# Summing ten modulation chunks on VectorE beside two projections, a narrower band mask and a one-step negated maximum

## The reference

```python
def modulation(cvec, w_ada, b_ada):            # w_ada: 1024 x 3072, layer 4: 1024 x 6144
    return jnp.split(jax.nn.silu(cvec) @ w_ada + b_ada, 3, axis=-1)

sh_l, sc_l, gt_l = modulation(c, w_ada, b_ada)       # latent tokens
sh_c, sc_c, gt_c = modulation(c_ctx, w_ada, b_ada)   # context tokens
h_l = rmsnorm(x_lat, g_pre) * (1.0 + sc_l[:, None, :]) + sh_l[:, None, :]
...
# window layers: 16 heads of 64, 4 key heads; |query - key| <= 128 among latents, all context keys
m = jnp.maximum(jnp.max(logits, axis=-1, keepdims=True), sink)
e = jnp.exp(logits - m)
return e / (jnp.sum(e, axis=-1, keepdims=True) + jnp.exp(sink - m))
```

## Time and profile before

| what | us |
| --- | --- |
| median of the timed runs (3) | 2514.43 (2513.34 to 2514.76) |
| the profiled execution | 2511.64 |
| its span | 2509.8 |
| TensorE busy in the span | 2363.6 (94%) |
| VectorE busy | 935.3 (37%) |
| ScalarE busy | 633.5 (25%) |
| projection of layer 0, from tile 4 on | 69.7 to 182.8 |
| attention of layer 0 | 183.8 to 312.5 |
| projection of layer 3, from tile 4 on | 1036.7 to 1109.3 |
| attention of layer 3 | 1110.2 to 1191.9 |

### The profile page before, as it was taken

How to read it: one execution, slowest core, us unless ns; L and a number is a source line. 1 busy time by engine, 2 the same in 40 slices (tenths; PEclk the granted TensorE clock), 3 DMA queues, 4 the chain that set the end, 5 groups by cost and what they waited for, 6 DMA issues and landing times. The chain is left out here.

```text
span 2509.8 us, 31515 instructions
## 1 busy us (share of the span) xinstructions
PE 2363.6 (94%) x11828; PEld 1264.7 (50%) x11829; DVE 935.3 (37%) x2112; ACT 633.5 (25%) x1450; POOL 45.8 (2%) x57
## 2 busy tenths in 40 slices
PE   7999899999999989999899789999999999999997
PEld 3545586468745557675786553333333333333332
DVE  2208643153600684436354433233223223322323
ACT  3016532343211353225331421111111111111111
POOL 0000000000000000000001000000000000000000
PEclk9999999999999999999999789999999999999999
DMA  9028921200122002249231049998998998998997
GB/s 337 34 90 316 350 79 42 72 32 34 68 68 73 28 2 101 101 147 356 68 135 67 21 194 369 417 417 343 417 417 348 417 417 348 418 418 350 418 418 306
DMA packets 154252, 568.00 MB, mean 226 GB/s; under 512 B 10832, under 2 KB 12368, under 8 KB 121136
## 3 DMA queue, kind: packets, MB, share of 16 engines
q1 hardware_dynamic: 154160, 566.75, 57.7%
HBM read 565.67 MB, written 1.05 MB: 226 GB/s over the span
## 5 line engine op out<-in xcount | busy, mean ns | idle before, releaser
L2495 PE MATMUL PS<-BIG,PW 128*64 128x512 f32 x2304 | 510.9, 598 | 11.0 <-DMA BIG<-in_w 10.9
L2495 PEld LDWEIGHTS PS<-BIG,PW 128*64 128x64 f32 x2304 | 160.8, 137 | 357.9 <-issue 322.1
L2521 PE MATMUL PS<-BIG,PW 128*64 128x512 f32 x1152 | 255.1, 595 | 8.6 <-ACT PW L2598 8.6
L2684 DVE TENSOR_SCALAR PW<-PS 128x512 f32<-128x512 f32 x36 | 24.9, 691 | 515.1 <-PE PS L2495 515.1
L2595 ACT ACTIVATE PW<-PW 128x512 f32<-128x512 f32 x36 | 22.7, 630 | 759.1 <-DVE PW L2684 759.1
L2521 PEld LDWEIGHTS PS<-BIG,PW 128*64 128x64 f32 x1152 | 79.3, 137 | 161.3 <-issue 144.1
L973 PE MATMUL PS<-HT,BIG 128*128 128x512 f32 (+1 forms) x448 | 154.0, 502 | 0.0
L619 PE MATMUL PS<-HT,BIG 128*128 128x256 f32 x640 | 139.5, 379 | 2.1 <-PEq L730 2.1
L619 PEld LDWEIGHTS PS<-HT,BIG 128*128 128x128 f32 x640 | 121.4, 190 | 19.1 <-issue 2.7
L973 PEld LDWEIGHTS PS<-HT,BIG 128*128 128x128 f32 x448 | 85.6, 191 | 62.6 <-issue 56.9
L1306 PE MATMUL PS<-BIG,HT 128*128 128x512 f32 x256 | 110.0, 592 | 0.0
(11 more groups left out here) (463 smaller groups left out, 3102.6 us busy)
## 6 DMA issues: line engine op xcount, KB each, us to landing
BIG<-in_w SPq DMA_DIRECT2D x384, 1024.0 KB, 15.8
BIG<-in_l_w_ada SPq DMA_DIRECT2D x24, 2048.0 KB, 9.2
BIG<-in_l_w_in SPq DMA_DIRECT2D x20, 2048.0 KB, 8.1
BIG<-in_w_ada SPq DMA_DIRECT2D x12, 2048.0 KB, 9.9
BIG<-in_l_w_out SPq DMA_DIRECT2D x8, 2048.0 KB, 10.0
BIG<-in_w_in SPq DMA_DIRECT2D x7, 2048.0 KB, 8.5
BIG<-in_w_out SPq DMA_DIRECT2D x2, 2048.0 KB, 7.8
BIG<-in_l_w_in SPq DMA_DIRECT2D x1, 1792.0 KB, 13.4
```

The costliest lines, as they stand in the source:

```text
L2495: ins = nc.tensor.matmul(PS[64 * g:64 * g + 64, 4 + half, :], xt[:, c % 4, c // 4, :], W[:, c, half * F + g * 512:half * F + g * 512 + 512 ...
L2521: ins = nc.tensor.matmul(PS[64 * g:64 * g + 64, 7, :], at_[:, k % 4, k // 4, :], W[:, 8 + k // 2, k % 2 * D + g * 512:k % 2 * D + g * 512 ...
```

## The change

1. **Ten chunks of each attention's modulation move into the projection block ahead of it.** Their weights no longer pass through the ring: SyncE loads them into two places of the arena (`load`), a load waiting until the chunk two before is summed. VectorE multiplies each 128-row slice k with a column of the condition and adds up over k (`sum_rows`): in layer 0 two rows per chunk (16 operations of 128x512), in layer 3 one row in two halves (8 operations). It does so in portions between its rope steps and after the key copies. TensorE adds over the partitions with a column of ones (`reduce`, four matmuls of 256 columns), each reduction at a fixed place behind a tile. The attention keeps ten late chunks in layer 0 and two in layer 3.
2. **The band mask** is added only to the 128 of 256 latent keys where it can be other than 0. The last layer's mask keeps its width.
3. **The negated maximum** with the sink is one operation, min(-scale x max, -sink), with the negated sink made once per attention.

```diff
+                if j >= 2:
+                    sp.wait_ge(*at("early_summed", j - 1))
+                sp.dma_start(self.places[j], t[ADA[l]][:, c * CH:(c + 1) * CH].rearrange("(k p) n -> p k n", p=P)).then_inc(
+                    S[f"early_loaded{j % 2}"].sem, 16)
...
+            def sum_rows(self, dve, a, b):
+
+                for x in range(a, b):
+                    j, k = x // KT, x % KT
+                    two = self.job[j][0] < 4
+                    if k == 0:
+                        dve.wait_ge(*at(f"early_loaded{j % 2}", 16 * (j // 2 + 1)))
+                        if j >= 2:
+                            dve.wait_ge(*at("early_reduced", j - 1))
+                    for h in range(2) if two else [k % 2]:
+                        sums = PART[:, j % 2, h, :]
+                        w, c = self.places[j][:, k, :], 27 + (h if two else 2)
+                        if k == 0 or (k == 1 and not two):
+                            ins = nc.vector.tensor_scalar(sums, w, COND[:, k, c:c + 1], None, ALU.mult)
+                        else:
+                            dve.wait_ge(dve_chain.sem, self.mark[h])
+                            ins = nc.vector.scalar_tensor_tensor(sums, w, COND[:, k, c:c + 1], sums, ALU.mult, ALU.add)
+                        if k == KT - 1 and h == 1:
+                            ins.then_inc(S["early_summed"].sem, 1)
...
+            def reduce(self, pe, j):
+                pe.wait_ge(*at("early_summed", j + 1))
+                for h in range(2):
+                    row = 3 * j + (h if self.job[j][0] < 4 else 2)
+                    for half in range(2):
+                        g = 32 * (2 * h + half)
+                        ins = nc.tensor.matmul(PS[g:g + 32, self.bank, 0:256], UNIT[:, 31 - row:63 - row],
+                                               PART[:, j % 2, h, half * 256:half * 256 + 256], start=(j == 0),
+                                               stop=(j == self.early - 1), tile_position=(0, g))
+                ins.then_inc(S["early_reduced"].sem, 1)
...
-                    x = j * (slots - 2 - 2 * self.batches) // len(self.job) + 2 * b
+                    x = 3 + (j - self.early) * (slots - 8) // late
...
+                pool_chain.link(pool, nc.gpsimd.memset(UNIT[:], 0.0))
+                pool_chain.add(nc.gpsimd.memset(UNIT[:, 31:32], 1.0))
...
                         if sink is not None:
                             h = 2 * units[i][0]
-                            dve_chain.link(dve, nc.vector.scalar_tensor_tensor(
-                                mx[:, i % 2, 2:4], mx[:, i % 2, 0:2], scale, sink[:, h:h + 2], ALU.mult, ALU.max))
-                            nc.vector.tensor_scalar(nm[:, i % 2, 0:2], mx[:, i % 2, 2:4], -1.0, None, ALU.mult).then_inc(
-                                S["max_ready"].sem, 1)
+                            nc.vector.scalar_tensor_tensor(nm[:, i % 2, 0:2], mx[:, i % 2, 0:2], -scale, minus_sink[:, h:h + 2],
+                                                           ALU.mult, ALU.min).then_inc(S["max_ready"].sem, 1)
...
+            sums_beside = [2, 1, 2, 1] + [4] * 6 if i == 0 else [0] * 4 + [3] * 4 + [8] * 2
+            reduced_behind = [4, 6, 8, 10, 13, 15, 16, 17, 19, 20] if i == 0 else [8, 9, 10, 12, 13, 15, 17, 18, 20, 21]
...
+                    if pending:
+                        ws.load_until(sp, first)
+                        for j in range(EARLY):
+                            mods.load(sp, j)
+                            if j in (3, 5):
+                                ws.load_until(sp, first + (j - 1) // 2)
+                    else:
+                        ws.load_until(sp, first - 1)
+                        mods.load(sp, 0)
+                        mods.load(sp, 1)
+                        ws.load_until(sp, first + 1)
+                        mods.load(sp, 2)
+                        sp.wait_ge(*done[3])
+                        for j in range(3, 6):
+                            mods.load(sp, j)
+                        ws.load_until(sp, first + 2)
+                        for j in range(6, EARLY):
+                            mods.load(sp, j)
                     ws.load_until(sp, first + 5)
...
                         if 1 <= j <= len(roped):
                             rope(j - 1)
+                        if j in reduced_behind:
+                            mods.reduce(pe, reduced_behind.index(j))
...
                         act.wait_ge(*done[j])
+                        if kind == "z" and m == 0 and not pending:
+                            act.wait_ge(*at("early_summed", 2))
...
+                    x = 0 if pending else 4
+                    mods.sum_rows(dve, 0, x)
                     for n, j in enumerate(roped):
                         kind, m, _, _, _ = tiles[j]
                         dve.wait_ge(*at("tile_taken", j + 1))
                         rope_turn(dve, (qt if kind == "q" else kt_)[:, m, :], n, tmp)
+                        mods.sum_rows(dve, x, x + sums_beside[n])
+                        x += sums_beside[n]
...
+                    mods.sum_rows(dve, x, KT * EARLY)
...
+            def masked(u):
+                x = P - u[1] * P
+                return (x, window[:, u[1], x:x + P]) if u[1] < 2 else None
```

More of the change, by code:

```diff
@@ L255, in layers_and_experts_kernel @@
                 ws.add("l1_w_ukv", t["l1_w_ukv"])
[L256 to L259, removed]
+            for l, c in {0: [(2, 2), (3, 0)], 3: [(4, EARLY)]}.get(i, []):
+                ws.add(ADA[l], t[ADA[l]][:, c * CH:])
+                ws.first[ADA[l]] -= c
             ws.add(f"l{i}_w_out", t[f"l{i}_w_out"])
@@ L265, in layers_and_experts_kernel @@
         ws.first["end"] = len(ws.chunks)
[L267 to L272, removed]
+        BESIDE = {0: [(l, c) for l in range(4) for c in range(4 if l == 0 else 0, 6)], 3: [(4, c) for c in range(12)]}
         dve_chain = Chain(ctx.enter_context(nc.semaphore("dve_chain")))
@@ L297, in layers_and_experts_kernel, with __init__, ring @@
         class Modulations:
-            def __init__(self, job, rows, bank, batch):
+            def __init__(self, job, rows, bank, batch, early=0, places=None):
                 self.job, self.rows, self.bank, self.batch = job, rows, bank, batch
-                self.end = job[-1][2] + 1
+                self.early, self.places, self.mark = early, places, [0, 0]
                 self.batches = -(-len(job) // batch)
+            def ring(self, j):
+                l, c = self.job[j]
+                return ws.first[f"l0_w_ada_{c}"] if l == 0 else ws.first[ADA[l]] + c
@@ L345, in take @@
                 while j < end:
-                    l, c, _ = self.job[j]
+                    l, c = self.job[j]
                     n = 1
-                    while j + n < end and self.job[j + n][0:2] == (l, c + n):
+                    while j + n < end and self.job[j + n] == (l, c + n):
                         n += 1
@@ L499, in layers_and_experts_kernel @@
         early = consts_at["eps"][1]
-        low, high = ([(0, c, ws.first[f"l0_w_ada_{c}"]) for c in cs] for cs in ((0, 2), (1, 3)))
-        mods = Modulations(low, arena.take(256), 7, 2)
+        mods = Modulations([(0, 0), (0, 2)], arena.take(256), 7, 2)
         w_first = BIG[:, RING_N + ARENA_N - KT * CH:].rearrange("p (k n) -> p k n", k=KT)
@@ L733, in _ @@
                 def _(sp):
-                    ws.load_until(sp, mods.end if mods else ws.done)
+                    ws.load_until(sp, mods.ring(len(mods.job) - 1) + 1 if mods else ws.done)
                 @block.tensor
@@ L873, in modulate @@
                                 mods.take(dve, j)
+                    if sink is not None:
+                        dve_chain.link(dve, nc.vector.tensor_scalar(minus_sink, sink, -1.0, None, ALU.mult))
                     maxima(0)
@@ L2223, in hybrid_mixer @@
             ws.done = c_in + 8
-            attention(units, 0.125, score, value, lambda u: dilated[:, u[1], 0:(u[1] + 1) * P], None, gate)
+            attention(units, 0.125, score, value, lambda u: (0, dilated[:, u[1], 0:(u[1] + 1) * P]), None, gate)
             first = ws.first["w_out_2"]
```

54 lines of the change are left out of this document (39 added, 15 removed).

## The result

The changed kernel takes 2536.1 us (median of 4 runs, 2528.47 to 2540.33), the kernel before beside it 2513.89: ratio 1.0088 [1.006, 1.0117], 22.2 us slower. The profiled execution is the fastest of the four, 2528.47 with a span of 2526.4; that of before had 2509.8.

What follows compares the result with a forecast made beforehand. TensorE was taken to bound the kernel. Projections +24.8 and +21.2, attentions -17.8 and -18.3, clock +5 made +15 on the profiled 2511.64, 2526.5; with 2.8 to the median, 2529 us, range 2511 to 2543.

Steps and rivals of the forecast that it cites:

- the four stages: Projection and attention of layers 0 and 3: +24.8, -17.8, +21.2, -18.3 us, with +5 for low clock, together +15.
- The waits: TensorE's queue in both projections stands at reductions until VectorE's last sum: 20.1 us in layer 0, 16.5 in layer 3.
- Loads bind in layer 3: Layer 3's projection: two load places, 7.9 us issue to landing, hold up the sums; +21.2 us, +15 without that limit.
- A reduction: Ten per projection in TensorE's queue, 0.47 us each, 4.7 us per projection; at most twice that.
- The clock: Low TensorE clock after three long waits, 2 to 2.5 us each: +5, bounds 0 and 8; chance 8 in 10.
- The attentions: Attentions of layers 0 and 3, ten chunks fewer each and shorter VectorE units: -17.8 and -18.3 us.
- The sums: VectorE's multiply-and-add operations beside the projections: 0.66 us start to start; a chunk 10.0 us in layer 0, 4.8 in layer 3.
- It cancels: Attentions give 22 and 20 us, layer 3's loads do not bind, clock stays: -2, 2512; chance 0.20.
- The attentions fall to TensorE's own work: TensorE's waits for VectorE ahead of the transposes vanish, all idle 10.4 and 6.8 us: -14.7, 2500; chance 0.12.
- Clearly slower: Projections: clock falls at every long wait, reductions cost double or sums 0.7 us: +25 to +30, 2541; chance 0.16.
- my sum: The prediction's main case for the whole kernel: 2529 us, range around it alone 2521 to 2538; chance 0.52.

Runs made afterwards that it cites:

- Experiment 3: The changed kernel with each reduction put a few tiles later, nothing else: 2512.78 us, ratio 0.9999 to the kernel before.
- experiment 8: The changed kernel with later reductions, ten chunks in both layers, and layer 3's z weights issued ahead of loads 2 to 9: 2508.96 us, ratio 0.9983.
- experiment 5: The changed kernel with unneeded filler matmuls ahead of the long waits (4, 4, 7, 1 in layer 0; 4, 4, 4 in layer 3): 2531.83 us, ratio 1.0076.
- experiment 10: The changed kernel run and profiled once more, unaltered: 2536.77 us, ratio 1.009 to the kernel before.

## Why the prediction was right, and where its sizes were off

It forecast 2529, slower, in a range of 2511 to 2543; measured were 2536. Sign and mechanism are right; the four stages sum to +22.0 where it had +15.

- **The waits** ("the step that decides"). Forecast 0.9, 4.3, 4.3, 6.9, 2.6, 1.1 us in layer 0; the trace has 0.81, 4.15, 4.15, 6.82, 0.90, 0.36. The brackets count from the end of the rope's matmul; counted by starts, as the forecast did, the long ones are 4.3. The two short ones came out shorter as slower tiles had made TensorE later. In layer 3 two of 4.15 and one of 4.44, at the chunk whose load was held up. In layer 3's later part, where the forecast had 7.9 us of waits in six pieces, they came as 4.44 and 0.28. Experiment 3 shows that in layer 0 the waits are the loss: 23.0 of the 30.2 us go with the places alone.
- **Loads bind in layer 3.** Forecast, and shown twice: experiment 3 takes away the early waits and gains 1.2 us there, experiment 8 ends in waits of 5.31 and 7.01, while eight chunks have none. The forecast put layer 3 without that limit at +15; with eight chunks and the later places of the reductions it is +5.6, since the early waits go as well. That the z weights came early enough held in the changed kernel only because the waits had delayed the tiles.
- **A reduction** was mis-sized: 0.47 us, a quarter of a chunk, in the sum; in the queue it costs 0.77 (experiment 3: 7.64 against 6.87). It is 0.57 up to the start of the tile behind it (96.96 to 97.53), and the rows around it make up the rest. Where nothing waits, ten of them make layer 0's projection 7.1 us longer (121.21 against 114.07; 0.6 comes back at the meeting of the engines, where TensorE idles 0.35 and not 0.94), not 4.7. That is 2.4 of the missing 7, and about all by which layer 0 with the clock kept up (experiment 5, +26.9) lies above 24.8.
- **The clock**: forecast +5. Experiment 5 gives 5.2 in the two projections and 2 to 4 in the timed runs, so the term holds in its place and is rather large for the whole. The clock fell behind all three long waits of layer 0 (0.50 in 139 to 141) and behind both in layer 3 (0.50 in 1085 to 1087, 0.56 in 1096 to 1098). In layer 0 the whole gain of 3.3 us is there when the third wait ends, 66.3 us behind tile 4 in place of 69.5, and stays 3.3 to the end: the first two falls cost 1.6 us each, less than the 2 to 2.5 that I took, and the third is absorbed, as I had said. In layer 3, where I had counted one, the two together cost 1.9. The page "TensorE: Matmul & The Clock Gate" of the Trainium skill, section "Why this matters for your kernels", advises against idle gaps between matmuls; here it agrees (0.66 and 0.53 behind 4.15 us, 1.00 with the gap filled), at a price of 5.2 us beside the 30 us of waits.
- **The attentions** give 16.65 and 17.4 in place of 17.8 and 18.3, 2.0 less together. A unit came out as counted (3.30 forecast 3.3, 4.97 forecast 4.97, a short one 2.34 forecast 2.3), so by elimination the difference lies at heads and tails; where exactly stays open. The second profile gives 15.6 for layer 0: its last mixing takes 1.12 us instead of 0.66.
- **The loads of layer 3** are the rest. With the clock kept up (experiment 5) that projection lies at +24.0, 2.8 above 21.2. It ends with VectorE's last sum, so a dearer reduction mostly comes out of the waits there. Counted from tile 4, VectorE ends chunk 3 after 52.9 us where the forecast had 52.4, and chunk 9 after 96.4 where it had 93.0: the loads fall behind the sum step by step. In the changed kernel load 6 stands out, which I had let follow the weight chunk at 5.2 us: issue when chunk 4 is summed, first product by the forecast 12.1 us later (1095.1 to 1107.2), measured 15.0.
- **The sums** took 0.66 us from start to start, as taken from the earlier trace rows. The halved throughput that the Trainium skill's "Vector Engine (DVE) Microarchitecture Reference", section "Points that are easy to get wrong", would give did not show; by the estimate of some 70 us more in layer 0 no version run here would have gained.
- **The rivals.** *It cancels* needed loads that do not bind and attentions at -42; the loads bound, and the attentions gave -34. *The attentions fall to TensorE's own work* did not happen: TensorE still idles 11.7 and 7.5 us there. *Clearly slower* came nearest beside my sum: its price was +25 to +30, and reductions dearer than counted, one of its conditions, came in part (0.77, not 0.94).

That the profiled run read +16.6 by the span and the medians +22 is mostly the clock of the other stages: from the second attention to the end the granted clock is 0.98 and TensorE is busy 1241 us in this profile, 0.97 and 1245 us both before and in experiment 10, with the same number of records. The prediction moved from a profiled run to the median with before's 2.8 us; for the changed kernel it was 7.6.

## What to carry to other kernels

Before an instruction is put into the queue of the engine that bounds, write down when its producer is done by the producer's own queue: a reduction a tile or two too early cost 4.3 us twice and 7.0 once in layer 0 and made the idea a loss; the same work one or two tiles later, with as many chunks in layer 3 as two load places can feed, is a gain of 0.7%. Count issue to landing against the number of places before choosing how much to move. Edits on an engine that does not bound are small until the bound is gone: mask and maximum were worth some 4 us alone, not clear of noise, and 10.7 behind the sums.

## What the hardware showed that I had not expected

- Four 32-column f32 matmuls of 256 columns in four column groups take 0.57 us from start to start when they stand alone, against 0.47 for a quarter of the sixteen in a row; 1.01 at the low clock. Between full tiles they make the queue 0.77 us longer.
- Nine full f32 matmuls of 512 columns leave 18 records and take 7.89 us, 0.87 each.
- The mean granted clock of the whole program moves between executions from 0.965 to 0.974 for the same kernel, and 12 us with it. Between the two profiles (0.967 and 0.974, 9.1 us) 6.8 us of that lie outside the four stages. The filled version spread over only 3.3 us in six runs, the changed kernel over 10 to 12. Whether the filler did that is open: layer 0's projection did not differ between the two profiles of the changed kernel.
